# Sample softmax one pair ahead of its values, and the last expert block's rows summed, normed and scattered by themselves

## The chip, the cores and the metric

One core of a Trainium2 chip runs the whole program. The metric is device time in microseconds (us), the median of several runs. TensorE (PE) does matmuls and transposes, with a queue of its own for weight loads (PEld); VectorE is DVE, ScalarE is ACT, GpSimd is POOL, SyncE (SP) issues most transfers. POOL issues the indirect ones, whose row numbers come from a tile. PE works at one of two clock levels, 1.2 and 2.4 GHz, and the profile gives the granted share of 2.4 GHz.

## What is computed

A one-layer decoder step on 1024 prompt rows and 64 sample rows (8 sequences of 8 new tokens, each with a cache of 1024 earlier positions). Attention has two groups of heads: A (4 query heads on 2 key heads, window 128, a learned sink) and B (6 heads, three dilated windows). Then an output projection, a norm, a mixture of 16 experts (each token goes to 2), and a final norm.

```python
def mixer_sample(h, ca_k, ca_v, cb_k, cb_v, conv_state, w_in, conv_w, sinks, table):
    ...
    oa, lse_a = gather_attention(qa, jnp.concatenate([ca_k, ka], axis=1),
                                 jnp.concatenate([ca_v, va], axis=1), idx, dist, table[:, :A_Q_HEADS])
    oa = apply_sinks(oa, lse_a, sinks)
    ...
    ob = dilated_sample(qb, jnp.concatenate([cb_k, kb], axis=1), jnp.concatenate([cb_v, vb], axis=1),
                        cb_k.shape[1], table[:, A_Q_HEADS:])
    ...
    mix = jnp.concatenate([oa.reshape(Bn, T, A_Q_W), ob.reshape(Bn, T, B_W), oc], axis=-1)

# in reference(), for the sample rows (the prompt rows likewise)
    ys = ys + ms @ w_out[l]
    ys = ys + hier_moe(rmsnorm(ys, norm_ffn[l]), ...)   # 2 of 16 experts of width 512 a token
    y_sample = rmsnorm(ys, norm_final)
```

## The kernel before

Four stages run one after the other, with a barrier between them: `project_in`, `attend`, `mix_out` (output projection, norm, router) and `experts` (with the final norm at its end). Within a stage each engine runs an order written out by hand, and semaphores alone tie the engines together. The change touches the end of `attend` and the end of `experts`.

**End of `attend`: the sample rows.** The 8 sequences go in 4 pairs `r`, two sequences in the two halves of the 128 partitions. For a pair PE turns the cached keys (36 transposes of 128x128, L1267, into the PSUM tiles `turn` and `score`, taken to `kT_s` by ACT and DVE at L858 and L860), makes the scores (12 matmuls, L1276), turns the softmaxed scores (7 transposes in two groups of 4 and 3, `sprobs`, L1316), multiplies them with the cached values (L1325, L1327), and later turns the result (`sout`, L1302). DVE adds the bias and finds the maximum (L1140), ACT takes the exponent (L971), DVE scales (L1144, L1145), ACT takes the values out of PSUM (L1028). Group A's scores, `aprobs` transposes and values (L1293 with the cached values, 128 partitions deep, and L1294 with the new ones, 8 deep, turn about for the 8 sequences) stand between the scores of pair 0 and the keys of pair 1. PE's order for pair `r` is: keys of `r`+1, scores of `r`+1, `sout` of `r`-1, `sprobs` of `r`, values of `r`. ACT takes the exponent of a pair behind the first half of the next pair's keys, and behind the values copy of the pair before. SP loads keys and values (two buffers each; the last two value tiles go to the key buffers) and, between keys 3 and 4, the whole of `w_out` (4 MB).

**End of `experts`.** 24 blocks of 128 token rows run one after the other, at least one an expert. POOL gathers the rows of a block from `h_rows` (`landing`), DVE copies them (`rows`, L2043), PE turns them and makes gate, up and down products; ACT and DVE split the weights of the next expert into two parts (L1823, L1828). At the end of a block ACT and DVE scale half of the sums each into `y_out` (L2018, L2075), once the block before has been stored (`y_stored`), and POOL adds `y_out` to the rows of `x1_rows` in memory by an indirect accumulating transfer (L1976). When the last block has been added, SP loads all 9 row tiles of `x1_rows` (`x1[t]`, L1944), ACT squares and roots (L2031, L2034), DVE inverts and scales (L2091, L2093), SP stores.

```python
            total = sp.value_load(ends[0:1, NE:NE + 1], min_val=NE, max_val=MAXB)
            sp.wait_ge(y_stored, 16 * total)
            for t in range(TT):
                n = tokens(t)
                sp.dma_start(x1[t][0:n, :], io["x1"][P * t:P * t + n, :]).then_inc(x_loaded[t], 16)
```

Of the kernel before, what the change touches and what calls it, by code (L numbers as in the profile page):

```python
# [22 lines left out]
I32 = mybir.dt.int32  # L23
# [6 lines left out]
P = 128  # L30
# [604 lines left out]
def attend(nc, io, keep):  # L635
# [9 lines left out]
    with ExitStack() as stack:  # L645
# [232 lines left out]
        def _(sp):  # L878
# [27 lines left out]
            def load_v(b):  # L906
                if b == 1:
                    sp.wait_ge(valued, DUOS)
                    sp.dma_start(va_cache[:, :, :], io["cache_a_v"]).then_inc(va_loaded, 16)
# [31 lines left out]
            sp.wait_ge(w_out_loaded, 80)  # L941
# [26 lines left out]
        def _(act):  # L968
# [44 lines left out]
            take_all(act, 0, "aprobs")  # L1013
            for r in range(PAIRS):
                take_all(act, 0, "ks", 2 * r + 2)
# [9 lines left out]
                act.wait_ge(valued, DUOS + 1 + r + 1)  # L1025
                if r:
                    act.wait_ge(turned, groups_of("sout", r - 1)[0] + 1)
                nc.scalar.activation(values_s[:, :], value[0][:, 0:BW], ACT.Copy).then_inc(values_taken, 1)  # L1028
# [3 lines left out]
        def _(dve):  # L1032
# [103 lines left out]
            for r in range(PAIRS):  # L1136
# [5 lines left out]
                take_keys(2 * r + 2)  # L1142
                dve.wait_ge(exped, UNITS + 2 + r + 1)
                step(nc.vector.reciprocal(recip[:, col:col + 1], denom[:, col:col + 1]))  # L1144
                nc.vector.tensor_scalar(probs[:, r % 2, 0:SK], probs[:, r % 2, 0:SK], recip[:, col:col + 1], None, ALU.mult).then_inc(scaled, 1)  # L1145
                take_keys(2 * r + 3)
# [13 lines left out]
        def _(pe):  # L1160
# [94 lines left out]
            def keys(r):  # L1255

                if r == PAIRS:
                    return
                buf = score[(r + 1) % 2]
# [9 lines left out]

                wait_taken(pe, groups_of("ks", 2 * r + 1)[-1])  # L1270
# [10 lines left out]
            keys(0)  # L1281
# [991 lines left out]
```

## Time and profile before

| | us |
|---|---|
| median of 3 runs (1153.05 to 1156.83) | 1154.96 |
| the profiled execution | 1156.61 |
| its span, first to last instruction | 1154.8 |
| `attend`, group A's values of the sample rows to the last `sout` | 447.3 to 522.4 |
| `experts`, end of the last down product | 1120.2 |
| from there to the end | 34.6 |

The profiled execution is 1.65 us above the median; its span is 1.8 us under its own time. Times in the rows are counted from the start of the span. In a row of a timeline stand the start, the busy time, the engine, the line and operation, output and inputs with their shape, the number of instructions merged, and in brackets the idle time just before with what ended it. PE is busy over 9 tenths of nearly every slice of the span; the exceptions are the start, the slices from 433 to 549 us and those after 1120 us.

### The profile page before, as it was taken

How to read it: one execution, taken by the hardware profiler on the slowest of the kernel's cores; microseconds unless marked ns; L12 is line 12 of the kernel's file. 1: busy time of each engine (PE TensorE's matmuls, PEld its weight loads, DVE VectorE, ACT ScalarE, POOL GpSimd, SP SyncE). 2: the span in 40 equal slices, each digit the busy share in tenths (PEclk: the TensorE clock that was granted, in tenths of full speed). 3: DMA queues.
4: the chain of work that ended last, by engine and by line, in shares of the span. 5: the costliest groups of instructions: out<-in, count | busy, mean ns of one | idle time of the engine just before them, and what ended most of it. 6: DMA issues, size and time to landing. Idle time of an engine off the chain costs nothing. (4 is left out here: it accounts for less than half of the span.)

```text
span 1154.8 us, 16329 instructions
## 1 busy us (share of the span) xinstructions
PE 1045.9 (91%) x5907; PEld 856.7 (74%) x5908; DVE 591.5 (51%) x971; ACT 480.5 (42%) x746; POOL 144.6 (13%) x135
## 2 busy tenths in 40 slices
PE   4999999999999988877999569999999999999970
PEld 4779999998766656446888458888887878888860
DVE  4421441110366653225355755665599966559744
ACT  5321100011466652224233343455468655547434
POOL 0000000000100000001000021221234422222430
PEclk9999999999999998988999769999999999999995
DMA  6325121102440009756322665668799966879629
GB/s 211 128 79 219 55 56 55 57 1 92 123 133 1 2 6 297 233 166 204 110 110 100 219 246 199 187 224 290 247 392 393 377 217 226 290 249 392 194 62 337
DMA packets 104161, 207.34 MB, mean 180 GB/s; under 512 B 12648, under 2 KB 47249, under 8 KB 104075
## 3 DMA queue, kind: packets, MB, share of 16 engines
q1 hardware_dynamic: 96764, 179.89, 44.3%
q0 software_dynamic: 7344, 26.74, 8.9%
q8 instruction: 33, 0.54, 0.2%
q14 instruction: 20, 0.16, 0.0%
HBM read 175.75 MB, written 36.55 MB: 184 GB/s over the span
## 5 line engine op out<-in xcount | busy, mean ns | idle before, releaser
L605 PE MATMUL bank<-xT_hi,w_hi 128*128 128x384 f32 (+1 forms) x432 | 94.7, 327 | 0.0
L605 PE MATMUL bank<-xT_rest,w_hi 128*128 128x384 f32 (+1 forms) x432 | 94.0, 326 | 0.0
L605 PE MATMUL bank<-xT_hi,w_rest 128*128 128x384 f32 (+1 forms) x432 | 94.0, 326 | 0.0
L1976 POOL DMA_INDIRECT x_rows<-y_out,out_id x24 | 60.2, 2510 | 182.4 <-DVE rows L2043 168.3
L1828 DVE TENSOR_TENSOR down_rest<-w_down,down_hi 128x2048 fp32r<-128x2048 f32 x32 | 71.9, 2287 | 18.8 <-ACT down_hi L1823 17.9
L2108 PE MATMUL gate<-gate_hi,rowsT_hi 128*128 128x512 f32 x192 | 76.8, 400 | 0.7 <-ACT rowsT_hi L1990 0.7
L2109 PE MATMUL gate<-gate_rest,rowsT_hi 128*128 128x512 f32 x192 | 77.4, 403 | 0.0
L2143 PE MATMUL y<-down_hi,hidT_hi 128*128 128x512 f32 x192 | 77.0, 401 | 0.0
L2109 PE MATMUL up<-up_rest,rowsT_hi 128*128 128x512 f32 x192 | 75.8, 395 | 0.0
L1828 DVE TENSOR_TENSOR gate_rest<-w_gate,gate_hi 128x2048 fp32r<-128x2048 f32 x32 | 73.1, 2283 | 4.7 <-ACT gate_hi L1823 4.7
L2108 PE MATMUL up<-up_hi,rowsT_hi 128*128 128x512 f32 x192 | 75.3, 392 | 0.0
L2144 PE MATMUL y<-down_rest,hidT_hi 128*128 128x512 f32 x192 | 74.9, 390 | 0.0
L605 PEld LDWEIGHTS bank<-xT_hi,w_rest 128*128 128x128 f32 x432 | 73.0, 188 | 0.0
L605 PEld LDWEIGHTS bank<-xT_hi,w_hi 128*128 128x128 f32 x432 | 72.8, 188 | 0.2
L605 PEld LDWEIGHTS bank<-xT_rest,w_hi 128*128 128x128 f32 x432 | 72.3, 188 | 0.0
L1828 DVE TENSOR_TENSOR up_rest<-w_up,up_hi 128x2048 fp32r<-128x2048 f32 x32 | 71.8, 2284 | 0.6 <-PEq L1338 0.6
L1823 ACT ACTIVATE down_hi<-w_down 128x2048 fp32r<-128x2048 f32 x32 | 59.7, 1916 | 13.2 <-issue 13.2
L1823 ACT ACTIVATE up_hi<-w_up 128x2048 fp32r<-128x2048 f32 x32 | 61.3, 1920 | 4.9 <-DMA w_up<-in_w_up 4.9
L1823 ACT ACTIVATE gate_hi<-w_gate 128x2048 fp32r<-128x2048 f32 x32 | 61.1, 1909 | 3.0 <-DMA w_gate<-in_w_gate 3.0
L980 ACT ACTIVATE logit<-logit,neg_max 128x256 f32<-128x256 f32 (+7 forms) x80 | 52.2, 656 | 6.3 <-DVE neg_max L1051 6.3
L860 DVE COPY probsT<-turn 128x256 f32<-128x256 f32 (+4 forms) x60 | 28.5, 496 | 43.1 <-PE turn L1189 26.0
L2061 DVE TENSOR_TENSOR hid<-up,silu 128x128 f32<-128x128 f32 (+1 forms) x48 | 18.1, 418 | 62.0 <-PE up L2112 62.0
(288 smaller groups left out, 2083.6 us busy)
## 6 DMA issues: line engine op xcount, KB each, us to landing
w_gate<-in_w_gate SPq DMA_DIRECT2D x16, 2048.0 KB, 12.8
w_up<-in_w_up SPq DMA_DIRECT2D x16, 2048.0 KB, 13.0
w_down<-in_w_down SPq DMA_DIRECT2D x16, 2048.0 KB, 14.1
stage<-in_w_in SPq DMA_DIRECT2D x6, 1536.0 KB, 6.9
k_cache<-in_cache_b_k SPq DMA_DIRECT2D x8, 768.0 KB, 6.6
bias_scratch<-bias_one_row SPq DMA_DIRECT2D x1, 5800.0 KB
mixT<-in_x_prompt SPq DMA_DIRECT2D x8, 512.0 KB, 3.8
x<-in_x_prompt SPq DMA_DIRECT2D x8, 512.0 KB, 4.3
```

The source lines that it names most:

```text
L605: ins = nc.tensor.matmul(bank[3 * (n % 2) + i][:, 0:m], w_tiles(wt, n // CH + 1)[:, k, cols], xt[:, k, c:c + m], start=(k == 0 and x == 0) ...
L860: ins = nc.vector.tensor_copy(out, src)
L980: nc.scalar.activation(logit[:, u % 4, 0:n], logit[:, u % 4, 0:n], ACT.Exp, bias=neg_max[:, u:u + 1], scale=-1.0, accum_out=denom[:, u:u + ...
L1823: self.nc.scalar.activation(self.hi[which][half][:, k, :], self.raw[which][half][:, k, :], ACT.Copy).then_inc(self.hi_made, 1)
L1828: self.nc.vector.tensor_tensor(self.rest[which][half][:, k, :], self.raw[which][half][:, k, :], self.hi[which][half][:, k, :].bitcast(F32) ...
L1976: nc.gpsimd.indirect_dma_start(out=io["x1"], out_offset=bass.IndirectOffsetOnAxis(ap=out_id[:, :], axis=0), in_=y_out[:, :], in_offset=Non ...
L2061: nc.vector.tensor_tensor(hid[:, cols], up[:, cols], silu[:, cols], ALU.mult).then_inc(hid_ready, 1)
L2108: nc.tensor.matmul(out[:, :], rowsT_hi[:, k, :], hi[:, k, :], start=(k == 0), stop=False)
L2109: nc.tensor.matmul(out[:, :], rowsT_hi[:, k, :], rest[:, k, :], start=False, stop=False)
L2143: nc.tensor.matmul(y[j][:, :], hidT_hi[:, k, :], moe.hi["down"][half][:, k, cols], start=(k == 0), stop=False)
L2144: nc.tensor.matmul(y[j][:, :], hidT_hi[:, k, :], moe.rest["down"][half][:, k, cols], start=False, stop=False)
```

## The change

In `attend`: the sample scores get their own function on PE, so that the scores of pair `r`+1 stand behind the `sprobs` transposes of pair `r` and ahead of its values; the exponent goes ahead of the values copy and of the next keys on ACT, the scaling ahead of the next keys on DVE; group A's values run first over the cached and then over the new values; SP loads 5 of 8 `w_out` parts ahead of keys 2, the rest behind keys 5.

In `experts`: the eviction of a block (`store_sums`) moves from the end of its step to the head of the next, behind the counts read there, and waits for `y_free`, which POOL raises after `y_stored`. The last block is not added in memory: SP loads the 9 tiles once the block before the last is stored, the norm of tiles 0 to 2 runs beside the last block's down product, and then the last block's sums are added in SBUF to the gathered rows (`last_x`), normed as a tenth tile, and scattered into the two outputs over the plain tiles.

```diff
@@ SP in attend
-            for b in (0, 1):
-                load_k(b)
-            for b in (0, 1):
-                load_v(b)
-            for b in (2, 3):
-                load_k(b)
+            load_k(0)
+            load_k(1)
+            load_v(0)
+            sp.wait_ge(valued, DUOS)
+            sp.dma_start(va_cache[:, :, :], io["cache_a_v"]).then_inc(va_loaded, 16)
             sp.wait_ge(heads_normed, 2 * QT_N)
...
-            sp.dma_start(w_out[:, 2:KD, :], io["w_out"][2 * P:, :].rearrange("(k p) c -> p k c", p=P)).then_inc(w_out_loaded, 16)
+            load_w_out(2, 5)
+            load_k(2)
+            load_k(3)
+            load_v(1)
             for r in range(1, PAIRS):
                 if r + 1 < PAIRS:
                     load_k(2 * r + 2)
                     load_k(2 * r + 3)
+                if r == 1:
+                    load_w_out(5, KD)
                 load_v(2 * r)
                 load_v(2 * r + 1)
@@ ACT in attend
+            def take_values(r):
+                act.wait_ge(valued, DUOS + 1 + r + 1)
+                if r:
+                    act.wait_ge(turned, groups_of("sout", r - 1)[0] + 1)
+                nc.scalar.activation(values_s[:, :], value[0][:, 0:BW], ACT.Copy).then_inc(values_taken, 1)
+
             for r in range(PAIRS):
-                take_all(act, 0, "ks", 2 * r + 2)
                 act.wait_ge(biased, UNITS + 2 + r + 1)
...
                 exp(r, UNITS + r, SK, None)
+                if r:
+                    take_values(r - 1)
+                take_all(act, 0, "ks", 2 * r + 2)
                 take_all(act, 0, "ks", 2 * r + 3)
@@ PE in attend
-            for b in range(NB):
-                out = value[1][:, 32 * b:32 * b + 32]
-                cols = slice(32 * (b % 4), 32 * (b % 4) + 32)
-                nc.tensor.matmul(out, va_cache[:, b, :], probsT[:, b // 4, 0, cols], start=True, stop=False)
-                ins = nc.tensor.matmul(out, va_new[:, b, :], probsT[0:NT, b // 4, 1, cols], start=False, stop=True)
+            for old in (True, False):
+                for b in range(NB):
+                    cols = slice(32 * (b % 4), 32 * (b % 4) + 32)
+                    ins = nc.tensor.matmul(value[1][:, 32 * b:32 * b + 32], va_cache[:, b, :] if old else va_new[:, b, :],
...
@@ experts: ACT (DVE likewise, with fetch(b + 1) behind it), POOL, SP
+            def store_sums(ahead):
+                act.wait_ge(downed, ahead)
+                act.wait_ge(y_free, ahead)
+                nc.scalar.activation(y_out[:, 0:512], y[0][:, :], ACT.Copy, scale=slot_w[:, bass.ds(ahead, 1)]).then_inc(y_act, 1)
...
+            for t in range(TT):
+                if t == 3:
+                    store_sums(total)
+                act.wait_ge(x_loaded[t // 3], 48)
+                root(t, tokens(t), x1[t][0:tokens(t), :])
+            act.wait_ge(last_added, 1)
+            root(TT, P, y_out[:, :])
...
+            nc.gpsimd.indirect_dma_start(out=last_x, out_offset=None, in_=io["x1"],
+                                         in_offset=bass.IndirectOffsetOnAxis(ap=out_id[:, :], axis=0)).then_inc(last_gathered, 16)
+            pool.wait_ge(last_number, 1)
+            pool.wait_ge(last_scaled, 1)
+            pool.wait_ge(out_stored, 16 * TT)
+            for rows_of, numbers, n in (("y_prompt", out_id, SEQ), ("y_sample", sample_id, NB * NT)):
+                nc.gpsimd.indirect_dma_start(out=io[rows_of], out_offset=bass.IndirectOffsetOnAxis(ap=numbers[:, :], axis=0),
+                                             in_=y_out[:, :], in_offset=None, bounds_check=n - 1, oob_is_err=False).then_inc(last_stored, 16)
...
-            sp.wait_ge(y_stored, 16 * total)
+            last = sp.value_load(ends[0:1, NE + 1:NE + 2], min_val=NE - 1, max_val=MAXB - 1)
+            sp.wait_ge(y_stored, 16 * last)
@@ experts: DVE after the loop
+                if t == 3:
+                    store_sums(total)
+                    dve.wait_ge(y_act, total)
+                    dve.wait_ge(y_dve, total)
+                    dve.wait_ge(last_gathered, 16)
+                    nc.vector.tensor_tensor(y_out[:, :], y_out[:, :], last_x, ALU.add).then_inc(last_added, 1)
```

One small step in `mix_out` (DVE) writes the number of blocks less one into `ends`, and `slot_w` is stored one column further right.

On PE, at group A's values of the sample rows, this stood before (the last two rows go on for all 8 sequences):

```order
L1294 MATMUL turn<-ident,logit 8x128
L1293 MATMUL value<-probsT,V 128x32 [waits sink_ready,va_loaded,dve_turned,act_turned]
L1294 MATMUL value<-probsT,va_new 128x32
L1293 MATMUL value<-probsT,V 128x32
L1294 MATMUL value<-probsT,va_new 128x32
```

and this stands there now:

```order
L1294 MATMUL turn<-ident,logit 8x128
L1302 MATMUL value<-probsT,V 128x32 [waits sink_ready,va_loaded,dve_turned,act_turned]
L1302 MATMUL value<-probsT,V 128x32 x7
L1302 MATMUL value<-probsT,va_new 128x32 x8
L1272 MATMUL turn<-ident,k_cache 128x128 [waits act_turned,dve_turned,k_loaded0,biased]
```

The 8 deep ones and the 8 shallow ones now stand together. On PE, behind the last keys of pair 1, before:

```order
L1267 MATMUL score<-ident,k_cache 128x128 x2
L1276 MATMUL score<-kT_s,q_blk 64x512 [waits new_k,dve_turned,act_turned]
L1276 MATMUL score<-kT_s,q_blk 64x512 x5
L1276 MATMUL score<-kT_s,q_blk 64x264 x6
L1316 MATMUL turn<-ident,logit 128x128 [waits dve_turned,act_turned,scaled]
L1316 MATMUL turn<-ident,logit 128x128 x3
L1316 MATMUL turn<-ident,logit 128x128 [waits dve_turned,act_turned]
L1316 MATMUL turn<-ident,logit 128x128
L1316 MATMUL turn<-ident,logit 8x128
L1325 MATMUL value<-v_cache,probsT 64x384 [waits v_loaded0,v_loaded1,dve_turned,act_turned]
```

and now:

```order
L1272 MATMUL score<-ident,k_cache 128x128 x2
L1327 MATMUL turn<-ident,logit 128x128 [waits dve_turned,act_turned,scaled]
L1327 MATMUL turn<-ident,logit 128x128 x3
L1327 MATMUL turn<-ident,logit 128x128 [waits dve_turned,act_turned]
L1327 MATMUL turn<-ident,logit 128x128
L1327 MATMUL turn<-ident,logit 8x128
L1283 MATMUL score<-kT_s,q_blk 64x512 [waits new_k,dve_turned,act_turned]
L1283 MATMUL score<-kT_s,q_blk 64x512 x5
L1283 MATMUL score<-kT_s,q_blk 64x264 x6
L1338 MATMUL value<-v_cache,probsT 64x384 [waits v_loaded0,v_loaded1,dve_turned,act_turned]
```

The scores of pair 1 went from ahead of the transposes of pair 0's softmax to between them and the values. On ACT, at the end of the last block (`rowsT_hi` belongs to its down product), before:

```order
L1990 ACTIVATE rowsT_hi<-turn 128x512 [waits turned5]
L2017 REGISTER_ALU [waits downed]
L2018 ISA [waits y_stored]
L2018 ACTIVATE y_out<-y,slot_w 128x512
L1908 REGISTER_ALU
L1908 COMPARE_AND_BRANCH
L1907 UNCONDITIONAL_BRANCH
L2025 ACT_TABLE_LOAD
L2025 ACTIVATE statsf<-epsf 128x1 [waits eps_setf]
L2031 ACTIVATE w_down,statsf<-w_gate 128x1024 [waits x_loadedf0]
```

and now:

```order
L2067 TENSOR_LOAD ends
L2067 ISA x2
L2069 ACT_TABLE_LOAD
L2069 ACTIVATE statsf<-epsf 128x1 [waits eps_setf]
L2074 ACTIVATE w_down,statsf<-w_gate 128x1024 [waits x_loadedf0]
...
L2077 ACTIVATE statsf<-statsf,epsf 128x1 [waits rootedf,squaredf]
L2037 ISA [waits y_free,downed]
L2037 ACTIVATE y_out<-y,slot_w 128x512
L2074 ACTIVATE w_down,statsf<-w_gate 128x1024 [waits squaredf,x_loadedf1]
```

The wait for the last down product (`downed`) went behind the squares and roots of three tiles.

## Rows read from the trace of the kernel before

**Rows 1.** Stretches: us; busy of PE, PEld, DVE, ACT, POOL; PEclk; DMA share; GB/s.

```profile
448.00:450.00 2.00, 2.00 (x12) 1.80 (x12) 0.15 (x3) 0.00 (x0) 0.00 (x0) 0.89 1.03 237
...
458.00:460.00 2.00, 2.00 (x12) 2.00 (x11) 1.00 (x4) 1.79 (x4) 0.00 (x0) 0.55 0.85 348
...
498.00:500.00 2.00, 2.00 (x6) 0.47 (x4) 0.00 (x0) 0.00 (x0) 0.00 (x0) 0.50 1.06 374
```

**Rows 2.** PE's waits from 430 to 530 us: total us, times, longest.

```profile
PE value L1325 <- ACT probsT L858: 2.0, 3, 0.7
PE score L1267 <- DVE kT_s L860: 1.8, 2, 1.7
PE turn L1316 <- DVE logit L1145: 1.2, 1, 1.2
...
PE turn L1316 <- DVE mixT L860: 0.8, 1, 0.8
```

**Rows 3.** Timeline of PE's weight loads at the start of group A's values.

```profile
447.26 0.19 PEld L1293 LDWEIGHTS value<-probsT,V 128*128 128x128 f32 x1 [0.88 <-ACT probsT L858]
...
447.36 0.19 PEld L1293 LDWEIGHTS value<-probsT,V 128*128 128x128 f32 x1
447.59 0.18 PEld L1294 LDWEIGHTS value<-probsT,va_new 8*128 8x128 f32 x1
```

**Rows 4.** Timeline of PE: first keys and scores of pairs 1 and 2, scores of pair 3.

```profile
454.68 1.54 PE L1267 MATMUL turn<-ident,k_cache 128*128 128x128 f32 x6
...
462.34 4.13 PE L1276 MATMUL score<-kT_s,q_blk 128*64 128x512 f32 x24 [0.69 <-issue]
...
472.95 0.87 PE L1267 MATMUL score<-ident,k_cache 128*128 128x128 f32 x6
...
479.02 4.13 PE L1276 MATMUL score<-kT_s,q_blk 128*64 128x512 f32 x24 [0.70 <-issue]
...
497.42 5.77 PE L1276 MATMUL score<-kT_s,q_blk 128*64 128x512 f32 x24 [0.58 <-ACT kT_s L858]
```

**Rows 5.** Transfers issued from 405 to 530 us: KB each, us to landing.

```profile
stage<-in_w_out SPq DMA_DIRECT2D x1, 3072.0 KB, 16.6
```

**Rows 6.** The chain that ended last, from the last eviction on: start, us, what.

```profile
1120.42 0.76 DVE y_out L2075
...
1122.08 6.17 DMA x_rows<-y_out,out_id
1128.27 0.34 SPq L1944
```

**Rows 7.** Transfers issued from 1095 us on: the last store.

```profile
out_y_sample<-w_down SPq DMA_DIRECT2D x1, 256.0 KB, 6.7
```

**Rows 8.** Timeline of ACT and DVE in the last block and the final norm.

```profile
1115.09 1.08 ACT L1990 ACTIVATE rowsT_hi<-turn 128x512 fp32r<-128x512 f32 x2
...
1121.10 1.28 ACT L2025 ACT_TABLE_LOAD   x1
...
1132.14 1.06 ACT L2031 ACTIVATE w_down<-w_gate 128x1024 f32<-128x1024 f32 x1 [9.46 <-DMA w_gate<-x_rows]
...
1133.53 1.04 ACT L2031 ACTIVATE w_down<-w_gate 128x1024 f32<-128x1024 f32 x1
...
1133.92 1.28 DVE L2093 SCALAR_TENSOR_TENSOR w_gate<-w_gate,statsf,w_down 128x1024 f32<-128x1024 f32 x1
...
1135.39 1.06 ACT L2031 ACTIVATE w_down<-w_gate 128x1024 f32<-128x1024 f32 x1 [0.41 <-DMA w_gate<-x_rows]
```

**Rows 9.** Timeline of POOL: two accumulating scatters of the expert blocks.

```profile
1070.57 7.76 POOL L1976 DMA_INDIRECT x_rows<-y_out,out_id  x1 [5.94 <-DVE rows L2043]
...
1103.91 1.60 POOL L1976 DMA_INDIRECT x_rows<-y_out,out_id  x1 [8.76 <-DVE rows L2043]
```

**Rows 10.** Waits of ACT in the expert blocks, 560 to 1125 us.

```profile
ACT y_out L2018 <- DMA x_rows<-y_out,out_id: 7.8, 2, 3.9
```

**Rows 11.** Waits of PE in the expert blocks, 560 to 1125 us.

```profile
PE hturn L2133 <- DVE hid L2061: 3.4, 3, 1.7
```

More of the change, by code:

```diff
@@ L1024, in _ @@
                 take_all(act, 0, "sprobs", r)
[L1025 to L1028, printed above, removed]
+            take_values(PAIRS - 1)
             take_all(act, 0, "sout", PAIRS - 1)
@@ L1253, in _, with turn_keys @@
             ins.then_inc(scored, 1)
[L1255 to L1259, printed above, removed]
+            def turn_keys(r):
                 if r:
@@ L1306, in _ @@
             for r in range(PAIRS):
-                keys(r + 1)
+                if r + 1 < PAIRS:
+                    turn_keys(r + 1)
                 if r:
@@ L1383, in mix_out @@
         first_slot = p.sb("first_slot", [P, NE])
[L1384 removed]
+        ends_f = p.sb("ends_f", [P, NE + 2])
         slot_i = p.sb("slot_i", [P, TT, 2], I32)
@@ L1886, in experts @@
         norm_g, squares = spare[2][:, D:2 * D], spare[2][:, 2 * D:3 * D]
-        stats = p.sb("statsf", [P, TT, 3])
+        last_x = spare[2][:, 3 * D:4 * D]
+        stats = p.sb("statsf", [P, TT + 1, 3])
         eps = p.sb("epsf", [P, 1])
+        sample_id = p.sb("sample_id", [P, 1], I32)
         eps_set = p.sem("eps_setf")
         g_loaded = p.sem("g_loadedf")
-        x_loaded = [p.sem(f"x_loadedf{t}") for t in range(TT)]
+        x_loaded = [p.sem(f"x_loadedf{i}") for i in range(3)]
         out_stored = p.sem("out_storedf")
+        y_free = p.sem("y_free")
+        last_gathered = p.sem("last_gatheredf")
+        last_added = p.sem("last_addedf")
+        last_scaled = p.sem("last_scaledf")
+        last_stored = p.sem("last_storedf")
+        last_number = p.sem("last_numberf")
         squared = p.sem("squaredf")
@@ L1960, in gather @@
                                              in_offset=bass.IndirectOffsetOnAxis(ap=row_id[:, :], axis=0)).then_inc(gathered, 16)
+            nc.gpsimd.sem_inc(y_free, 1)
             gather(FIRST)
@@ L1970, in block_step @@
                     pool.wait_ge(y_stored, 16 * b)
+                    nc.gpsimd.sem_inc(y_free, 1)
                 nc.gpsimd.tensor_copy(out_id[:, :], slot_ids[:, bass.ds(b, 1)]).then_inc(id_copied, 1)
@@ L2049, in rows_lo, with store_sums @@
                                         hi.bitcast(F32), ALU.subtract).then_inc(rowsT_lo_made, 1)
+            def store_sums(ahead):
+                dve.wait_ge(downed, ahead)
+                dve.wait_ge(y_free, ahead)
+                nc.vector.tensor_scalar(y_out[:, 512:D], y[1][:, :], slot_w[:, bass.ds(ahead, 1)], None, ALU.mult).then_inc(y_dve, 1)
             def block_step(b, here=None, following=None):
+                if b is not FIRST:
+                    store_sums(b)
+                    fetch(b + 1)
                 if here:
@@ L2085, in _, with norm @@
             expert_loops(dve, block_step)
+            total = dve.value_load(ends[0:1, NE:NE + 1], min_val=NE, max_val=MAXB)
+            last = dve.value_load(ends[0:1, NE + 1:NE + 2], min_val=NE - 1, max_val=MAXB - 1)
+            nc.vector.tensor_scalar(sample_id[:, :], slot_ids[:, bass.ds(last, 1)], SEQ, None, ALU.bitwise_xor).then_inc(last_number, 1)
             dve.wait_ge(g_loaded, 16)
-            for t in range(TT):
-                n = tokens(t)
+            def norm(t, n, x):
                 dve.wait_ge(rooted, t + 2)
@@ L2092, in _ @@
                 dve.wait_ge(inverted, t + 1)
-                nc.vector.scalar_tensor_tensor(out=x1[t][0:n, :], in0=x1[t][0:n, :], scalar=stats[0:n, t, 2:3], in1=norm_g[0:n, :],
-                                               op0=ALU.mult, op1=ALU.mult).then_inc(scaled, 1)
+                return nc.vector.scalar_tensor_tensor(out=x, in0=x, scalar=stats[0:n, t, 2:3], in1=norm_g[0:n, :], op0=ALU.mult, op1=ALU.mult)
+            for t in range(TT):
+                if t == 3:
[4 more added lines that the diff above has]
+                    nc.vector.tensor_tensor(y_out[:, :], y_out[:, :], last_x, ALU.add).then_inc(last_added, 1)
+                norm(t, tokens(t), x1[t][0:tokens(t), :]).then_inc(scaled, 1)
+            norm(TT, P, y_out[:, :]).then_inc(last_scaled, 1)
         @block.tensor
```

64 lines of the change are left out of this document (34 added, 30 removed).

## Prediction

> **What bounds the kernel now.** I read the slices of the span first: PE is busy over nine tenths nearly everywhere, so outside the start, the sample attention and the end, only less work for PE or a higher clock would help. The change touches two of the three exceptions. In the table of 2 us stretches the sample attention looks full, but the granted clock is 0.89 at 448, falls to 0.55 by 458 (0.5 is the 1.2 GHz level) and is 0.50 again at 498 [rows 1]. PE's waits there are small and many: for `probsT` 2.0 us in 3 waits, for `kT_s` 1.8, for `logit` of the last pair 1.2, for `mixT` 0.8 [rows 2]. So this stage is bounded by PE with a stutter: each wait is PE waiting for what ACT or DVE make of its own last product. Two timelines give the price of each step: group A's values [rows 3], and the keys and scores of the pairs [rows 4]; the list of transfers tells how long `w_out` takes, 16.6 us for 3 MB [rows 5].
>
> The end is bounded otherwise. The chain of waits goes from the last eviction (1120.42) through the accumulating scatter (6.17 us to landing) to the first load of `x1` at 1128.27 [rows 6], and on through the norms to the last store, which takes 6.7 us to land [rows 7]; PE is idle in all of it. ACT waits 9.46 us for the first tile and starts its root at 1132.14; then a root follows every 1.39 us, and DVE ends a tile 3.06 us after its root began (1133.92 + 1.28 - 1132.14) [rows 8]. POOL, DVE and ACT in the 24 blocks are off the path: PE waits for `hid` in only 3 places there (below).
>
> **The change part by part: sample attention.** All sums are made against the profiled execution, 1156.61 us.
>
> (a) *Group A's values.* Before, they run from 447.26 [rows 3] to the keys of pair 1 at 454.68 [rows 4]: 7.4 us for 32 weight loads (8 sequences, twice deep and twice shallow, as fp32 goes in several passes). From one deep load to its twin the step is 0.10, from deep to shallow 0.23 [rows 3], so a change of depth costs 0.13. At full clock that would be 16 x 0.10 + 16 x 0.23 = 5.3; the other 2.1 is the clock, at or under 0.89 [rows 1]. With one change of depth it is 32 x 0.10 + 0.13 = 3.3. The keys behind took 7.66 to their scores (462.34 - 454.68, a wait of 0.69 in it), those of pair 2 at full clock 6.07 (479.02 - 472.95, wait 0.70) [rows 4]; without the waits 7.0 and 5.4. So before it is 7.4 + 7.0 = 14.4. Should the clock stay, 3.3 + 5.4 = 8.7, a gain of 5.7; should it fall in the same proportion, 3.3 x 7.4 / 5.3 = 4.6 and 7.0, a gain of 2.8. I take **3.5**, near the lower end, because nothing in the shallow loads themselves, the nearest rows, says that the fall goes away.
>
> (b) *Waits that get cover.* The scores of the next pair (4.13 us [rows 4]) now stand between the transposes of a pair and its values. The 2.0 us for `probsT` [rows 2] fall under them. The transposes in turn stand between the keys and the scores, so the 0.69 + 0.70 + 0.58 that scores waited for their last key bank [rows 4] fall under transposes. New is a wait of the transposes for a PSUM tile that the last keys have just filled: at most the same 0.6 three times, at least nothing; I take 0.6 in all, since ACT and DVE have the scaled exponent out of the way by then. Gain 2.0 + 2.0 - 0.6 = **3.4**.
>
> (c) *Keys of pair 3.* DVE's share of `kT_s` came 1.7 late [rows 2]; in the code of DVE the scaling of pair 2, which waits for ACT's exponent, stands among them. With the scaling ahead of the keys, and the exponent ahead of the values copy on ACT, this goes, with some 0.5 of the smaller waits: **2.2**, at least 0 should the scaling itself push the keys by as much.
>
> (d) *Last pair.* The 1.2 for its `logit` [rows 2] goes, as its exponent is no longer behind a values copy. But its second group of transposes still needs the `sout` tile taken out, a wait of 0.8 [rows 2] that stays or comes back. Net **0.4**.
>
> (e) *Clock in the scores of pair 3.* They took 5.77 against 4.13 [rows 4] at 0.50 [rows 1]; the engine had stood still 1.68 + 0.58 us in the keys just before. Without that pause the clock should hold: **1.6**, at least 0.
>
> (f) *Loads.* SP's new order puts 5 of 8 parts of `w_out` ahead of keys 2. Their only consumer, the output projection, stands behind the barrier that ends the stage. I cost it at nothing, covered by the work of PE on pairs 0 and 1, beside which the transfers run; without the cover it is a rival below.
>
> Sum: 3.5 + 3.4 + 2.2 + 0.4 + 1.6 = **11.1** (5 to 15).
>
> **Experts, the 23 boundaries.** The eviction moves to the next step's head, but on ACT and DVE it still stands between the same two pieces of work. Added is the wait for `y_free`: behind it on ACT and DVE are the next rows and weights, and PE waits for these. POOL raises it after its own scatter has landed and its queue has come to that point. For the last pair of blocks the scatter issued at 1103.91 [rows 9] lands at 1110.1 by 6.17 [rows 6], while the eviction comes at 1120.4 [rows 6]: ten us to spare. Cost **0**.
>
> **The end.** The last scatter and what hung on it is gone from the path; what is late next is ACT. SP may load once block 22 has landed, 1110.1. Before, the first root began 3.87 us after the load was issued (1132.14 - 1128.27) and the third at 7.12 (1135.39) [rows 8]; one semaphore stands for three tiles, so 1117.3. ACT is in the last block's `rowsT_hi` until 1116.2 and then loads its table, 1.28 [rows 8]; with the reading of a register (under 1.1) and the first small root, 1118.8. So the first root starts at **1118.8**, not at 1117.3. Roots 0 to 2 end at 1118.8 + 3 x 1.4 = 1123.0. Here is the added wait: the eviction of the last block, ready at 1120.2, stands behind three tiles on ACT and DVE. ACT evicts until 1123.7; DVE finishes tile 2 at 1118.8 + 2 x 1.4 + 3.1 = 1124.7, evicts 0.76 [rows 6] and adds, some 1.3 for 1024 columns like its other two-operand pass [rows 8]: 1126.8. Six more tiles at 1.4 bring DVE to 1135.2 and the tenth to 1136.6; the ninth store, issued at 1135.2, lands 3.7 later if nothing is queued (an estimate from 3.87 of the first loads), 6.7 as the last store before [rows 7]; I take 1138.9, since loads and stores no longer share the time. POOL then issues two scatters. The last one began 0.90 after its eviction ended (1122.08 - 1120.42 - 0.76) and landed 6.17 later [rows 6]: 1138.9 + 0.9 + 6.2 = 1146.0 for the first. The second is issued 1.6 later [rows 9], but writes only the sample rows, 64 of 1088, and I take it to land no later. With 0.4 to the end of the span, as behind the last store (1146.41 + 1.28 + 6.7 = 1154.4 [rows 6, 7]), the end is 1146.4 against 1154.8: a gain of **8.4** (3 if the two run one after the other, 12 if a plain scatter lands as fast as a load, 3.87, and the ninth store a us earlier).
>
> The trace has no plain scatter, only the accumulating one at 6.17. The Trainium skill ("DMA: Bandwidth & Descriptors", section "Anatomy of one DMA — SWDGE (gpsimd) path") prices a transfer of POOL's queue at 2.0 us and its bytes by 436 GB/s: an estimate of 3.2 us for 512 KB, by which the end would come 3.0 earlier. The accumulating row is nearly twice that, so the sum stays with the row.
>
> **Total.** 11.1 + 8.4 = 19.5: 1156.61 - 19.5 = 1137.1; the median (1154.96) lies 1.65 below this execution, so 1135.4, about **1135**.
>
> **Rivals.**
>
> *The clock stays low.* With the values of group A at half clock, and transposes behind them, the clock might not return before the first scores; then (a) brings only its depth changes, 2.0, and (e) nothing: 1.5 + 1.6 = 3.1 back, 1138.5. For it: 0.50 came twice already in this stage [rows 1]. Against: it came back from 0.55 at 458 to full by 460 with transposes alone running. The Trainium skill ("TensorE: Matmul & The Clock Gate", section "Part 4: PE-mode transpose") says that transposes don't count as PE work for the clock. By that rule moving transposes ahead of the scores prolongs the low stretch; the trace's return under keys alone disagrees. Chance 0.18.
>
> *`w_out` is in the way.* Half of the 3 MB that took 16.6 us [rows 5] now stands ahead of keys 2: 8.3 us. If half of that reaches the keys and values behind, whose buffers come free only as PE uses them, the sample part gives 4.2 back: 1139.6. For it: with faster pairs each transfer is due sooner. Against: the buffers come free earlier too. Chance 0.1.
>
> *Scatters in a row.* If the second only starts when the first has landed, the end is 6 later: 1141. Against: on this queue an issue takes 1.6, not 6, and nothing in the code stands between. Chance 0.12.
>
> *Slower: POOL's scatter holds the next eviction.* Most scatters are issued in 1.6, but some take 7.76 [rows 9], and then ACT waited for the landing, up to 3.9, though only twice in 24 blocks (7.8 in all) [rows 10]. If `y_free`, which comes only when POOL has worked its way to it, were late at nearly every boundary, PE would wait as it does for `hid` in 3 places, up to 1.7 each [rows 11]; 23 x 1.7 = 39, less the gain of 19.5: 1174. It turns the sign from 19.5 / 1.7 = 12 late boundaries. Against: a scatter of 7.76 takes 6.2 longer than the one of 1.60 for which ten us were to spare. Chance 0.04.
>
> *It doesn't do what it says.* The waits of (b) to (d) only move, as each softmax hangs on the same two engines, and the tail's eviction behind three tiles costs what it saves; the depth changes (15 x 0.13 = 2.0) and the 3 of the lower bound at the end are left: 1150. Chance 0.04.
>
> **How the numbers follow.** Forecast 1135, chance 0.52; with the rivals 1. The range of 8 in 10 takes in the bounds of the attention (5 to 15) and of the end (3 to 12), and leaves out both extremes together: 1128 to 1146; 1150 and 1174 are outside. What a measurement of this kernel can tell from no change is about 0.3%, 3.5 us: faster than that 0.94, within it 0.02, slower 0.04.
>
> **What would show it.** In the profile after: keys of pair 1 in under 6.5 us with a clock near 1 (a); no wait for `probsT` over 0.1 (b); no 1.7 for `kT_s` (c); scores of pair 3 in 4.1 to 4.2 (e); the first root of the norm some 1.4 us ahead of the end of the last down product, and two scatters overlapping. Wrong would be: waits of ACT or DVE for `y_free` of over a us at many boundaries; keys waiting for their transfer; an end more than 31 us after the last down product (34.6 before, 26.2 by the sum).

## The result: 8 us faster, not 20

The changed kernel took 1147.59 us (median of 9 runs, 1145.18 to 1154.47) against 1155.8 of before on the same chip: ratio 0.9939, interval 0.9915 to 0.9964. (A ratio is the time over that of the kernel before; behind it stands its 95% interval. This one is 7 us, from 4 to 10.) Measured again (the run `again` below) it was 0.9926, 0.9899 to 0.9954. The direction was forecast, the size was not: 1135 was forecast, and the range ended at 1146.

Of its two profiled executions (1154.47 and 1147.08 us) the second is near the median; the rows here are from it. What the prediction said of the sample attention can be checked in the timeline of PE (start, busy time, line, operation, in brackets the wait before):

```profile
450.19 1.94 PE L1302 MATMUL value<-probsT,V 128*128 128x32 f32 x16 [0.62 <-ACT probsT L858]
452.07 1.97 PE L1302 MATMUL value<-probsT,va_new 8*128 8x32 f32 x16
453.96 0.88 PE L1272 MATMUL turn<-ident,k_cache 128*128 128x128 f32 x6
...
460.48 4.13 PE L1283 MATMUL score<-kT_s,q_blk 128*64 128x512 f32 x24
...
495.56 4.13 PE L1283 MATMUL score<-kT_s,q_blk 128*64 128x512 f32 x24
```

Group A's values take 3.8 us (450.19 to 453.96) where they took 7.4 [rows 3, 4], and the scores of pair 3 take 4.13, not 5.77 [rows 4]. (In three other profiles with this order, `attn_only`, `aligned_drain` and `loads_undone`, the values take 5.3 to 5.6 us.) The clock still falls to 0.50, but beside the keys, and returns (us, busy times of five engines, clock, DMA share, GB/s):

```profile
452.00:454.00 2.00, 2.00 (x19) 1.92 (x18) 0.87 (x3) 0.04 (x1) 0.00 (x0) 1.00 1.07 319
456.00:458.00 2.00, 2.00 (x11) 1.93 (x10) 0.89 (x3) 0.88 (x2) 0.00 (x0) 0.50 1.07 297
458.00:460.00 2.00, 2.00 (x18) 2.00 (x17) 1.30 (x3) 1.08 (x3) 0.00 (x0) 0.85 0.90 237
```

PE's waits there, answering to [rows 2] (total, times, longest):

```profile
PE value L1338 <- DMA v_new<-out_b_v_sample: 5.2, 2, 3.2
PE turn L1327 <- ACT mixT L858: 1.4, 2, 0.8
...
PE value L1338 <- ACT probsT L858: 0.6, 1, 0.6
```

The waits for `probsT` went from 2.0 to 0.6 (the last pair, which has no next scores), that of 1.7 for `kT_s` and the one for `logit` are gone. In their place PE waits 5.2 us for value tiles that have not landed (7.5 in the first profile): this wait was not in the sum. Behind both waits the clock is down again, beside the values of pairs 1 and 2:

```profile
484.00:486.00 2.00, 2.00 (x10) 0.87 (x8) 0.00 (x0) 0.00 (x0) 0.00 (x0) 0.52 1.11 260
```

```profile
504.00:506.00 2.00, 2.00 (x8) 0.90 (x6) 0.00 (x0) 0.00 (x0) 0.00 (x0) 0.50 1.09 267
```

So these values take 5.3 and 5.7 us (483.23 to 488.56, 501.70 to 507.41), and those of pair 0, at full clock, 4.0.

At the end the last down product and the first root of the norm:

```profile
1116.03 2.01 PE L2214 MATMUL y<-down_hi,hidT_lo 128*128 128x512 f32 x8
```

```profile
1116.08 1.06 ACT L2074 ACTIVATE w_down<-w_gate 128x1024 f32<-128x1024 f32 x1 [0.45 <-DMA w_gate<-x_rows]
```

The root begins 2.0 us ahead of the end of the down product (1118.0); the forecast had 1.4. From there the kernel takes 27.3 us to its end at 1145.3 (before 34.6, by the sum 26.2). The two scatters (POOL's timeline, then KB and us to landing from the list of transfers) and what stands behind them (instructions of the line that closes the stage: shortest, median and longest ns, first and last start):

```profile
1136.48 1.01 POOL L2022 DMA_INDIRECT out_y_prompt<-y_out,out_id  x1 [26.64 <-issue]
1137.80 1.00 POOL L2022 DMA_INDIRECT out_y_sample<-y_out,sample_id  x1 [0.30 <-issue]
```

```profile
out_y_prompt<-y_out,out_id POOLq DMA_INDIRECT x1, 3.3
out_y_sample<-y_out,sample_id POOLq DMA_INDIRECT x1, 2.7
```

```profile
L1852 POOLq DRAIN  x1: 4317/4317/4317, 1140.8 to 1140.8; - x1
```

The scatters land after 3.3 and 2.7 us, the later one at 1140.5, and then POOL drains for 4.3 us, in which no other engine has work left. Before, the same instruction stood where nobody saw it, 25 us ahead of the end:

```profile
L1838 POOLq DRAIN  x1: 4230/4230/4230, 1129.8 to 1129.8; - x1
```

### The profile page after: what moved, and what is told of

Its sections match the earlier page's. It is cut to its first block and busy times, and to the rows that moved or that the text cites. A ratio compares the mean times of both kernels' runs of the same rounds, so it can differ in the third digit from the quotient of the medians.

```text
span 1152.7 us, 16360 instructions
## 1 busy us (share of the span) xinstructions
PE 1046.5 (91%) x5907; PEld 856.9 (74%) x5908; DVE 594.3 (52%) x975; ACT 481.7 (42%) x749; POOL 146.9 (13%) x135
## 5 line engine op out<-in xcount | busy, mean ns | idle before, releaser
L2210 PE MATMUL y<-down_rest,hidT_hi 128*128 128x512 f32 x192 | 75.1, 391 | 0.0
L2002 POOL DMA_INDIRECT x_rows<-y_out,out_id x23 | 48.9, 2128 | 177.3 <-DVE rows L2094 162.8
L1980 POOL COPY row_id<-slot_ids 128x1 int32 (+1 forms) x26 | 35.5, 1365 | 152.4 <-POOLq L1351 139.9
```

The source lines that it names most:

```text
L1980: nc.gpsimd.tensor_copy(row_id[:, :], slot_ids[:, bass.ds(b, 1)]).then_inc(gather_id, 1)
L2002: nc.gpsimd.indirect_dma_start(out=io["x1"], out_offset=bass.IndirectOffsetOnAxis(ap=out_id[:, :], axis=0), in_=y_out[:, :], in_offset=Non ...
L2210: nc.tensor.matmul(y[j][:, :], hidT_hi[:, k, :], moe.rest["down"][half][:, k, cols], start=False, stop=False)
```

## Which half of the change missed

```diff
again:            the changed kernel
attn_only:        before + the hunks in attend
experts_only:     before + the hunks in mix_out and experts
w_out_as_before:  changed kernel, SP's order of loads in attend as before
```

What was expected of `again`:

> The changed kernel itself, a second time. Theory A (transfers): the attention's gain is lost to value tiles that land late (4.96 and 2.55 us of waits in the first profile, with the DMA queues full at about 250 GB/s), so another execution shows such waits again, together over 3 us, and the ratio is 0.993 again. Theory B (a bad execution): the first profile started group A's values 4.9 us late for reasons that lie before the change; a usual execution shows under 1 us of waits for value tiles and ends its sample attention 8 to 11 us earlier than before. Both: from the last down product to the end 29 us, with a 4.3 us drain of POOL as its last piece.

What was expected of `attn_only`:

> Kernel before with the change in the attention alone. If the ends' 5.6 us (34.6 to 29.0 in the first profile) are right, 2 to 3 us are left for the attention: ratio 0.998 (theory A). By the prediction's sum 11.1 us: 0.990.

What was expected of `experts_only`:

> Kernel before with the change in the experts alone. By the first profile 34.6 - 29.0 = 5.6 us: ratio 0.995. By the prediction's sum 8.4 us: 0.993. If y_free held evictions, the ratio would be over 0.998.

What was expected of `w_out_as_before`:

> The changed kernel with SP's order of loads as before (the whole of w_out behind keys 3, no part behind keys 5). Theory A with w_out in the way: the waits for value tiles go, 3 to 7 us faster than the changed kernel (ratio 0.987 to 0.990). Theory A with the queues full in any order: the waits move to other tiles, ratio 0.993 again. Theory B: no difference from the changed kernel within 2 us.

Measured: `again` 0.9926 (1146.98 us). `attn_only` 0.9914 (0.9886 to 0.9942), 9.9 us faster than before: the attention's 11.1 lies in the interval (6.7 to 13.2). `experts_only` 0.9978 (0.9963 to 0.9992): 2.5 us, though its profile has 28.1 us from the last down product to the end, 6.5 fewer than before. `w_out_as_before` 0.9906 (0.9878 to 0.9934), not to be told from `again`; its profile waits 4.6 us for value tiles. So my theory that the attention brought 2 or 3 us fell. The experts' change shortens the end and loses some 4 us (2 to 6 by the interval) somewhere else.

## Where the experts' change loses: addresses

Laid side by side, PE's instructions of the profiles with the experts' change are 1 to 2 us late behind the first loads of the program, where no code was changed (the 201st starts at 58.8 us before and at 60.2 in `again`).
```profile
w_gate<-in_w_gate SPq DMA_DIRECT2D x14, 2048.0 KB, 13.0
w_up<-in_w_up SPq DMA_DIRECT2D x14, 2048.0 KB, 13.0
w_down<-in_w_down SPq DMA_DIRECT2D x14, 2048.0 KB, 14.1
```

```profile
w_gate<-in_w_gate SPq DMA_DIRECT2D x14, 2048.0 KB, 13.7
w_up<-in_w_up SPq DMA_DIRECT2D x14, 2048.0 KB, 13.7
w_down<-in_w_down SPq DMA_DIRECT2D x14, 2048.0 KB, 14.7
```

```diff
shifted (before, and nothing else; 16 columns in pad64, 64 in pad256):
+        p.sb("spare_8", [P, 8])
aligned (changed kernel):
-                "ends": p.sb("ends", [P, NE + 2], I32), "slot_ids": p.sb("slot_ids", [P, MAXB + 3], I32),
+        numbers = p.sb("numbers", [P, NE + 2 + MAXB + 3], I32)
+        keep["ends"], keep["slot_ids"] = numbers[:, 0:NE + 2], numbers[:, NE + 2:]
```

What was expected of `shifted`:

> Kernel before with nothing but 32 unused bytes a partition allocated behind slot_w, which is what the larger slot_w of the change does to the addresses of 115 SBUF tiles (mixT, stage and all expert weights no longer begin on a multiple of 64 bytes). Theory C (placement): the four profiles with the experts' change are 1.0 to 1.7 us late after the first loads, 1.5 later at 410 us, and wait about 2 longer for the first rows of the experts; if the addresses do that, this kernel is 3 to 4.5 us slower than before: ratio 1.003 to 1.004. Theory D (chance, or another part of the experts' change): ratio 1.000.

What was expected of `aligned`:

> The changed kernel with ends and slot_ids in one tile, so that slot_w ends where it did and all other tiles have the addresses of before. Theory C: 3 to 4.5 us faster than the changed kernel, ratio 0.988 to 0.990. Theory D: as the changed kernel, 0.993.

What was expected of `pad64`:

> Kernel before with 64 unused bytes a partition in the place where shifted has 32. The expert weights then begin 64 bytes behind a multiple of 256. If only a start on a multiple of 64 counts: packets of 4096 bytes take 159 ns again (164 in shifted) and the ratio is 1.000. If a start on a multiple of 256 counts: 162 to 164 ns and 1.002.

What was expected of `pad256`:

> The same with 256 bytes. All theories by which the start of a tile counts: 159 ns, ratio 1.000. If it cost to move them at all: 164 ns and 1.002.

| run | ratio to before | interval | packets of 4096 and 2048 bytes, median ns, 700 to 1080 us |
|---|---|---|---|
| before | 1 | | 159, 84 |
| `shifted` | 1.0023 | 1.0008 to 1.0039 | 164, 86 |
| `pad64` | 1.0024 | 1.0007 to 1.0040 | 164, 86 |
| `pad256` | 1.0004 | 0.9990 to 1.0019 | 159, 84 |
| `again` | 0.9926 | 0.9899 to 0.9954 | 164, 86 |
| `aligned` | 0.9895 | 0.9874 to 0.9916 | 159, 84 |

(The packet times are worked out from the trace's packet records of the queue that SP's loads use.) The loads of `pad64` and `pad256`:

```profile
w_gate<-in_w_gate SPq DMA_DIRECT2D x14, 2048.0 KB, 13.7
```

```profile
w_gate<-in_w_gate SPq DMA_DIRECT2D x14, 2048.0 KB, 12.9
```

The start of the tiles counts: 2.7 us (0.9 to 4.5) in the kernel before. Moving them by 256 bytes costs nothing that shows. Between `again` and `aligned` it is 3.6, but their intervals overlap; only the packet times are clearly apart. My expectation of `shifted` had "a multiple of 64"; `pad64` shows that 64 is not enough. Between 64 and 256 nothing was tried. The Trainium skill ("DMA: Bandwidth & Descriptors", section "How a descriptor splits into AXI transactions") says that a transfer's piece is read in transactions that start at multiples of 256 bytes, so that one that starts off them begins at the boundary below and fetches bytes that it doesn't use. It says so of what is read; here the start of what is written moved. The runs show the price, 3% of a packet of 4096 bytes and 2% of one of 2048, and not whether this is the reason.

The expectation of `shifted` also put 2 us at the experts' first rows down to the addresses; its profile has them on time, so that was another cause (next but one section).

## The drain, and the parts of the attention

```diff
aligned_drain, aligned_drain_2 (aligned; POOL, then SP):
-            pool.wait_ge(last_stored, 32)
+            sp.wait_ge(last_stored, 32)
turns_undone (aligned_drain): group A's values turn about, as before
order_undone (aligned_drain): order of PE, ACT and DVE in the pairs as before
loads_undone (aligned_drain): SP's order of loads as before
w_out_last (aligned_drain; SP):
-                if r == 1:
-                    load_w_out(5, KD)
...
+            load_w_out(5, KD)
             sp.wait_ge(w_out_loaded, 96)
```

What was expected of `aligned_drain`:

> As aligned, and the wait for the landing of the two last scatters moved from POOL to SP. If the 4.3 us of POOL's DRAIN are a fixed price that begins when POOL has nothing left to wait for, it starts about 1.7 us earlier, beside the landing, and the tail is 1.7 us shorter than that of aligned (27.3 to 29.0 before, so 25.6 to 27.3), the time 1.5 to 2 us lower. If the drain waits for the transfers itself, nothing changes.

What was expected of `aligned_drain_2`:

> aligned_drain again, beside the next three on one chip: ratio 0.986 again, 15 to 18 us faster than before.

What was expected of `turns_undone`:

> aligned_drain with group A's values turn about, deep and shallow, as before. Step (a) of the prediction alone: 3.5 us (2.8 to 5.7) slower than aligned_drain_2, ratio about 0.989. If the keys behind are only waiting for their loads or the clock falls all the same, under 2 us.

What was expected of `order_undone`:

> aligned_drain with the order of before on PE, ACT and DVE in the sample pairs (scores ahead of the transposes, exponent behind the keys), but group A's values and SP's loads as changed. Steps (b) to (e) say 3.4 + 2.2 + 0.4 + 1.6 = 7.6 us slower than aligned_drain_2, ratio 0.993. Theory A (part of it came back as waits for value tiles, 2.7 to 5.2 us in the profiles): 3 to 5 us slower, ratio 0.989 to 0.991, with no such waits in its profile.

What was expected of `loads_undone`:

> aligned_drain with the loads of before on SP (the whole of w_out behind keys 3). Step (f) at nothing: as aligned_drain_2 within 1.5 us. If w_out ahead of keys 2 was what made the value tiles late: 2 to 3 us faster than aligned_drain_2 and no wait for value tiles over 1 us. If its two halves were right: slower, with waits for keys of pair 2 or 3.

What was expected of `w_out_last`:

> aligned_drain with the second part of w_out (1.5 MB) behind the last value tiles instead of behind keys 5. If the queues, full from 440 to about 503 us in the profiles of aligned_drain, are what makes value tiles late (3.1 and 3.4 us of waits there), the tiles land earlier, the waits fall under 1 us and the time is 2 to 3 us lower: ratio 0.984. If the tiles are late because their buffers come free late, nothing changes (0.9865), or w_out is now late for the output projection (0.988).

`aligned_drain` came to 0.9863 (0.9838 to 0.9887) and again to 0.9866 (0.9848 to 0.9885), against 0.9895 of `aligned` (the intervals overlap). From the last down product to the end its two profiles take 26.0 and 25.4 us, that of `aligned` 27.3: 1.3 and 1.9 less, where 1.7 was expected. All profiles agree: 25.1 to 26.0 in the eight with this wait on SP, 27.3 to 29.0 in the five with it on POOL. The drain now begins beside the scatters and is over 4.3 us after the last one was issued:

```profile
L1852 POOLq DRAIN  x1: 6042/6042/6042, 1128.8 to 1128.8; - x1
```

So it is a price that runs from POOL's last own work, not from the landing.

`turns_undone` 0.9884 (0.9867 to 0.9900): step (a) is worth some 2.1 us in the end; the interval overlaps that of `aligned_drain_2`, so the times alone don't prove it. In place it is worth more: from group A's values to the scores of pair 1 it is 14.7 us there and 11.0 in `aligned_drain_2`. What is lost again is about the 1.9 us that PE waits for keys that have not landed, a wait that `turns_undone` doesn't have. PE's waits from 446 to 523 us, `aligned_drain_2`:

```profile
PE value L1338 <- DMA v_new<-out_b_v_sample: 3.4, 2, 3.1
PE score L1272 <- DMA k_cache<-in_cache_b_k: 1.9, 2, 1.8
```

`order_undone` 0.9905 (0.9889 to 0.9922, clear of `aligned_drain_2`): steps (b) to (e) are worth some 4.5 us, not 7.6. Its profile has the waits of before, and none for a transfer:

```profile
PE value L1329 <- ACT probsT L858: 2.0, 3, 0.8
PE score L1269 <- DVE kT_s L860: 1.9, 2, 1.7
PE score L1278 <- issue: 1.4, 2, 0.7
PE turn L1320 <- DVE logit L1147: 1.2, 1, 1.2
```

The 3.1 us that are missing are less than the new waits for tiles, 3.4 and 1.9. The queues are full there (`aligned_drain_2`, stretches of 10 us, last columns clock, DMA share, GB/s):

```profile
470.00:480.00 10.00, 6.92 (x46) 3.62 (x44) 3.31 (x6) 3.75 (x13) 0.00 (x0) 1.00 1.05 268
480.00:490.00 10.00, 7.24 (x48) 4.34 (x49) 2.63 (x7) 1.97 (x5) 0.00 (x0) 1.00 0.97 234
490.00:500.00 10.00, 9.06 (x62) 5.26 (x62) 4.29 (x13) 2.86 (x5) 0.00 (x0) 1.00 1.08 288
```

`loads_undone` 0.9878 (0.9863 to 0.9894): without the new order of loads the waits are shorter (1.4 us for value tiles, 1.1 for keys), but the time is the same or 1.4 us longer, so that order isn't shown to cost anything. `w_out_last` 0.9850 (0.9827 to 0.9872), with 1.9 us of waits for value tiles and none for keys; its interval overlaps that of `aligned_drain_2`, so the 2 us that its waits promise stay unproved.

The traces do tell why a tile is late. SP may ask for the value tiles of pair 1 only when PE has finished the values of pair 0 and their buffers are free. SP's queue in `aligned_drain_2`, with the second part of `w_out` ahead of them:

```profile
459.56 0.51 SPq L919 DMA_DIRECT2D stage<-in_w_out  x1
...
467.20 1.18 SPq L913 DMA_DIRECT2D v_cache<-in_cache_b_v  x2
```

`w_out_last`, with it behind:

```profile
468.64 1.18 SPq L913 DMA_DIRECT2D v_cache<-in_cache_b_v  x2
...
493.81 0.37 SPq L919 DMA_DIRECT2D stage<-in_w_out  x1
```

In both PE is ready for these tiles 10.5 to 10.7 us after SP asks for them (at 477.9 and 479.15). In `aligned_drain_2` it then waits 3.1 us, in `w_out_last` not at all, and in `best` (below), which has the same order, at most 0.2; their waits of 1.9 and 1.3 are for the value tiles of pair 2. So the buffers leave only this much time in either kernel, and the transfers ahead in the queue decide whether it is enough.

## A copy that lost a race

```diff
experts_mended (experts_only with the repairs of aligned and aligned_drain), best (w_out_last); POOL:
-            nc.gpsimd.sem_inc(y_free, 1)
             gather(FIRST)
+            nc.gpsimd.sem_inc(y_free, 1)
```

What was expected of `experts_mended`:

> experts_only with three repairs: the addresses of before, SP waiting for the last scatters, and POOL's first raise of y_free behind the first gather instead of ahead of it. If that one instruction makes POOL's copy of row_id begin just behind DVE's first split (663.27 against 663.22 in the changed kernel; 667.98 against 668.00 before), the copy takes 0.18 instead of 2.28 us again and the first rows come 2.1 us earlier. The end in the profiles of aligned_drain is 25.4 to 26.0 us against 34.7 before: 8.7 to 9.3 us faster than before, ratio 0.992 (the prediction's term for the end was 8.4). Without the third repair working 0.994; experts_only was 0.998.

What was expected of `best`:

> w_out_last with POOL's first raise of y_free behind the first gather. If both add up, 0.983, 20 us faster than before, and a copy of 0.18; 0.985 and 2.28 if that instruction isn't the cause.

The first gather of the experts waits for POOL's copy of the row numbers. Before, POOL and DVE:

```profile
667.98 0.18 POOL L1956 COPY row_id<-slot_ids 128x1 int32<-128x1 int32 x1 [140.03 <-POOLq L1338]
```

```profile
668.00 2.30 DVE L1828 TENSOR_TENSOR up_rest<-w_up,up_hi 128x2048 fp32r<-128x2048 f32 x1 [0.55 <-PEq L1338]
```

Changed kernel (`again`):

```profile
663.27 2.29 POOL L1980 COPY row_id<-slot_ids 128x1 int32<-128x1 int32 x1 [139.94 <-POOLq L1351]
```

```profile
663.22 2.29 DVE L1842 TENSOR_TENSOR up_rest<-w_up,up_hi 128x2048 fp32r<-128x2048 f32 x1 [0.56 <-PEq L1351]
```

`best`:

```profile
658.88 0.18 POOL L1980 COPY row_id<-numbers 128x1 int32<-128x1 int32 x1 [140.10 <-POOLq L1350]
```

Before, POOL was 0.02 us ahead of a DVE operation; the raise of `y_free` ahead of the gather puts it 0.05 behind, and it takes as long as that operation. PE then waits 10.8 us for the first rows instead of 8.6. With the raise moved, the copy takes 0.18 again in both runs. It is so in all profiles: 2.28 or 2.29 in the eleven kernels with the raise ahead of the gather, 0.18 in the other seven. The Trainium skill ("SBUF — State Buffer", section "SBUF: two separate sides") describes such a lock between a DVE operation with two SBUF inputs and a GpSimd operation that reads SBUF, held for a whole instruction; the trace agrees, 2.29 beside 2.29.

`experts_mended` came to 0.9897 (0.9871 to 0.9923), 11.9 us faster than before (8.9 to 14.9), where `experts_only` was 2.5 faster. The three repairs, by the sections above 2.7 (addresses), 1.3 to 1.9 (drain) and some 2 (PE's wait for the first rows), make 6 to 7 of these 9.4; the rest is within the intervals. `best` came to 0.9831 (0.9807 to 0.9856), median 1136.43 us, 19.5 faster than before: the fastest of all. That this is what was forecast for the change itself is chance: `best` has four repairs that the prediction didn't have, and its parts are not those of the sum (next section).

## Why the prediction was wrong, step by step

Three profiles can be laid end to end, at points that PE's timeline shows. Each row is the length of a stretch, in us (sums are rounded; the 34.6 of above is 34.66 here):

| stretch | before | `again` | `best` | forecast | `again` less before |
|---|---|---|---|---|---|
| start to group A's values of the sample rows | 447.3 | 450.2 | 450.5 | 0 | +2.9 |
| from there to the last `sout` | 75.1 | 67.6 | 62.8 | -11.1 | -7.5 |
| to PE's first turn of expert rows | 152.8 | 154.9 | 153.0 | 0 | +2.1 |
| to the end of the last down product | 445.0 | 445.4 | 442.2 | 0 | +0.4 |
| to the end of the span | 34.7 | 27.3 | 25.4 | -8.4 | -7.4 |
| span | 1154.8 | 1145.3 | 1133.9 | -19.5 | -9.5 |

So of the 10 us that are missing in this execution, 3.6 are in the sample attention, 1.0 at the end and 5.4 in stretches that the prediction put at nothing.

**(a)** 3.5 forecast. In the profile of `again` values and keys take 453.96 + 5.7 - 450.19 = 9.4 us against 14.4, so 5.0; undone, 3.7 in place and 2.1 in the time. A weight load with its matmul took 0.12 us at full clock, not 0.10, so the values 3.8 and not 3.3. The reason given for the lower end was half right: the clock fell again, later and for less long. The rival of a clock that stays low did not come about: it is back before the scores (0.50 to 0.85 from 456 to 460 above), with transposes alone running.

**(b) to (e)** 7.6 forecast, 4.5 measured. The waits named in [rows 2] went much as written: of the 2.0 for `probsT` 1.4 fell under the scores (0.6 was the last pair's, which has none behind it), and the 0.8 for `mixT` in (d) stayed. The step that failed is "fall under them", together with (f) at nothing: PE gets to its values sooner than these land, and waits 5.2 us in `again`. The forecast of (f), that loads cost nothing because PE's work covers them, held for their order and failed for their amount: the DMA share was 1.03 and 1.06 in the rows of before already [rows 1]. The rival "`w_out` is in the way" came nearest, with 4.2 us: it named the keys and values behind and their buffers, but the first part of `w_out`, where the second made those of pair 1 late. In (e) the scores of pair 3 did run at 4.13, but 5.77 was no fixed price: of the seven profiles with the old order, three show 5.6 to 5.8 and four 4.1. In `again` the clock falls beside the values of pairs 1 and 2 instead.

**The experts' boundaries** at nothing: for `y_free` itself this held. ACT waited for POOL once, 4.2 us, three times in `aligned` and four in `best`, and PE has no wait that follows from it; the slower side did not come about. But nothing was too little to expect. Without the experts' change PE waits 2.5 to 4.4 us for `hid` (3.4 before [rows 11]), with it at the addresses of before 0 to 1.3 in seven of eight kernels and 2.2 in `loads_undone`. The blocks (fourth row) take 444.3 to 445.0 at these addresses without the change, and 442.0 to 443.6 with it, but 445.1 in `loads_undone`. In `again` and the three others with both the change and the shifted addresses, 2.1 to 2.3 of new waits stand there:

```profile
PE y L2209 <- ACT hidT_hi L2056: 2.2, 2, 1.2
```

Why the waits for `hid` went is not shown.

**The end** 8.4 forecast, and 7.4 in the profile of `again` (34.7 to 27.3); in the five profiles with this end it is 5.6 to 7.4. That it came near is luck, as two errors nearly cancelled. The scatters land after 3.3 and 2.7 us, not 6.17: of the two ends named, the accumulating row was the wrong neighbour, and the load (3.87) the right one. The estimate of 3.2 from the Trainium skill, which the prediction set aside, was met (the two scatters together wrote 0.49 MB). And "0.4 to the end of the span, as behind the last store" was taken from SP's last transfer; POOL now ends last, and its drain of 4.3 could have been read in the trace of before.

**Missing from the sum** were two costs on work that the change does not touch: 2.7 us for the addresses (0.9 to 4.5), and some 2 for the copy (10.8 - 8.6 = 2.2 in PE's wait). The addresses lie in the first stretch of the table (1.4 of its 2.9) and in the blocks (446.1 in `shifted`, 445.9 in `pad64`, 445.0 before). The other 1.5 of the first stretch are not the change's: the clock falls at about 411 us in 12 of the 18 profiles, of kernels with and without it, and before's is one of the six where it doesn't. Before, then `again`:

```profile
412.00:416.00 4.00, 3.95 (x27) 2.33 (x24) 3.67 (x10) 2.98 (x8) 0.00 (x0) 1.00 0.00 0
```

```profile
412.00:416.00 4.00, 4.00 (x24) 2.30 (x20) 2.53 (x5) 1.55 (x4) 0.00 (x0) 0.72 0.00 0
```

So a difference of 1.5 us between two executions need not come from the change. The place of the copy could have been found beforehand. PE's busy tenths in 40 slices of the span, before:

```profile
PE   4999999999999988877999569999999999999970
```

The 5 and the 6 are the slices from 635 to 693 us, at the end of `mix_out` and ahead of the first expert rows. The text ahead of the prediction lists as exceptions the start, the slices up to 549 us and the end, and the prediction went by that list: it passed over the slices in which PE is idle most between its start and its end. The range failed because it was built from the terms of the change alone, and none of the signs of being wrong that the prediction named stands in the profile of `again`, since they watch the changed parts alone.

## What to carry to other kernels

A change that makes a small tile longer moves everything behind it: compare the addresses of both programs, and try the kernel with the tiles back in their places (32 and 64 bytes off cost 2 to 3% of a packet here). Where an edit makes another engine the last one to finish, look up what that engine still does at its end in the trace of before. When a stage's DMA share is already 1, price saved PE time at what the transfers leave of it. And price the whole span: lay it out in stretches, before and after, and look for idle time also where nothing was changed.

## What the runs showed of the hardware that was not expected

- Loads into tiles that begin 32 or 64 bytes behind a multiple of 256: 164 ns a packet of 4096 bytes instead of 159, and 0.23% of the time of this kernel (0.08 to 0.39).
- POOL's drain at the end of its program takes 4.2 to 4.3 us and runs from its last own instruction.
- Two plain scatters that together wrote 120 rows of 4 KB landed 3.3 and 2.7 us after their issue, an accumulating one of 128 rows after 6.2 [rows 6].
- A POOL copy of 128 numbers takes 0.18 or 2.29 us, by 0.07 us of its start.
- The clock of the same code differs between executions: it falls at about 411 us in 12 of 18 profiles, for 1.5 us of time, and in the sample attention at changing places.
